# Expert layers of a tuned transformer kernel: a gather in fp32 straight from x, a fifth weight unit held aside, logits by token tiles, the gate bias as one row, and a last norm by halves

## The reference

```
x   = layer_norm(ALPHA * x + mix @ w_o[i])
aff = softmax(x @ router_w[i])                     # 256 tokens x 16 experts
gates, idx = top_k(aff.T, 32)                      # each expert takes its 32 best tokens
xg  = x[idx]                                       # 16 experts x 32 tokens
ffn = scatter_add(gates * ((silu(xg @ w1) * (xg @ w3)) @ w2))
ple = sigmoid(x @ ple_gate_w[i] + ple_gate_b[i]) * (p[i] @ ple_w[i])
x   = layer_norm(ALPHA * x + ffn + ple)
```

## Time and profile before

| | us |
|---|---|
| median of 3 runs | 2186.15 (2185.86 to 2186.26) |
| the profiled execution, its own time | 2185.28 |
| its span, first to last instruction | 2183.3 |
| PE busy | 1911.9, 88% |
| DVE, ACT busy | 1059.3, 712.3 |
| HBM read | 621.76 MB, 285 GB/s over the span |
| expert layer 0, in the profile | from about 128 to 609 |
| expert layer 1 | from about 711 to 1190 |

### The profile page before, as it was taken

One profiled execution on the slowest core, in us unless ns is written; L12 is line 12 of the kernel. 1 busy time (PEld: TensorE's weight loads), 2 busy tenths in 40 slices (PEclk: granted clock), 3 DMA queues, 4 the chain that ended last, 5 costly groups with the idle time before them and its releaser, 6 DMA issues. The chain is left out here.

```text
span 2183.3 us, 32580 instructions
## 1 busy us (share of the span) xinstructions
PE 1911.9 (88%) x13124; PEld 1354.3 (62%) x13140; DVE 1059.3 (49%) x1607; ACT 712.3 (33%) x1096; POOL 75.6 (3%) x137
## 2 busy tenths in 40 slices
PE   9999667676788986676768999999999999999998
PEld 6765224232366542242324888988888888888887
DVE  4761002010077500020103877787777877787776
ACT  5532002020046210020102433565444433565442
POOL 0000000000010000000000000000000000000000
PEclk9999989998999998898999999999999999999999
DMA  7399999999982899999999655436564655446550
GB/s 243 139 381 427 428 428 423 429 424 427 421 343 72 353 426 430 427 424 428 424 428 398 226 177 205 139 136 212 178 206 155 212 174 201 146 136 207 180 201 19
DMA packets 187952, 624.05 MB, mean 286 GB/s; under 512 B 17655, under 2 KB 129369, under 8 KB 163033
## 3 DMA queue, kind: packets, MB, share of 16 engines
q1 hardware_dynamic: 187864, 622.84, 73.6%
HBM read 621.76 MB, written 1.05 MB: 285 GB/s over the span
## 5 line engine op out<-in xcount | busy, mean ns | idle before, releaser
L3028 PE MATMUL psum<-x_both,up_hi 128*128 128x512 f32 x1408 | 352.9, 393 | 2.5 <-DVE x_both L525 2.2
L2275 PE MATMUL psum<-weight_ring,arena 128*32 128x256 f32 x3840 | 249.5, 411 | 106.7 <-DMA weight_ring<-in_w 106.1
L3028 PEld LDWEIGHTS psum<-x_both,up_hi 128*128 128x128 f32 x1408 | 257.4, 188 | 57.4 <-issue 3.3
L2275 PEld LDWEIGHTS psum<-weight_ring,arena 128*32 128x32 f32 x3840 | 123.5, 116 | 233.8 <-DMA weight_ring<-in_w 133.5
L2415 DVE TENSOR_TENSOR arena<-arena,psum 128x256 f32<-128x256 f32 x32 | 13.5, 421 | 450.6 <-PE psum L2275 450.6
L2297 PE MATMUL psum<-weight_ring,arena 128*32 128x512 f32 x1024 | 148.0, 709 | 73.6 <-DMA weight_ring<-in_w 63.6
L3080 DVE TENSOR_TENSOR up_lo<-weight_ring,up_hi 128x2048 fp32r<-128x2048 f32 x84 | 192.1, 2287 | 13.0 <-ACT up_hi L3051 12.8
L3031 PEld LDWEIGHTS psum<-x_both,up_lo 128*128 128x128 f32 x1408 | 189.4, 188 | 13.5
L3031 PE MATMUL psum<-x_both,up_lo 128*128 128x256 f32 x1408 | 193.2, 280 | 0.0
L3092 DVE TENSOR_REDUCE arena<-psum 128x256 f32<-128x512 f32 x176 | 121.5, 690 | 125.3 <-PE psum L3031 124.2
L652 PE MATMUL psum<-w_lo,x_both 128*128 128x384 f32 (+3 forms) x768 | 170.2, 359 | 2.4 <-DVE mix_lo L793 1.2
(11 more groups left out here) (390 smaller groups left out, 2393.7 us busy)
## 6 DMA issues: line engine op xcount, KB each, us to landing
weight_ring<-in_w SPq DMA_DIRECT2D x184, 2048.0 KB, 25.7
weight_ring<-in_ffn_wg SPq DMA_DIRECT2D x44, 1024.0 KB, 6.0
weight_ring<-in_ffn_wu SPq DMA_DIRECT2D x44, 1024.0 KB, 8.6
weight_ring<-in_ffn_wd SPq DMA_DIRECT2D x44, 1024.0 KB, 5.0
weight_ring<-in_w_in SPq DMA_DIRECT2D x14, 1536.0 KB, 6.7
weight_ring<-in_w_o SPq DMA_DIRECT2D x4, 2048.0 KB, 16.2
arena<-in_w SPq DMA_DIRECT2D x4, 2048.0 KB, 14.9
weight_ring<-in_ple_gate_w SPq DMA_DIRECT2D x4, 2048.0 KB, 25.0
```

The costliest lines, as they stand in the source:

```text
L2275: last = pe.matmul(ps[j * CAP:(j + 1) * CAP, 4 + k // 2, 0:QW], tokens[:, cc, :], w[c][:, j * QW:(j + 1) * QW], start=cc == 0, stop=cc == ...
L3028: last = pe.matmul(ps[:, 4 + 2 * f + h, :], w_part[:, f, h, c, :], x_both[:, :, c, :], start=c == 0, stop=False, skip_group_check=True)
```

## The change

Five edits. The gathers take x itself, in fp32, with eight elements between neighbours in the stationary operand, and one-hot matrices read as fp32; the first gather repeats its 64 columns twice, not four times. rows_hi and rows_lo are gone, and x_cols and ln_params hold a fifth aside unit, the first down unit of expert 1. Aside unit 0 is issued in `mix_out_norm`; the places of the ple inputs in the arena are moved for that. The columns for the logits are made tile by tile, and each tile has 24 products of 128 columns; two of the four ple products are made before them and two in the wait for the ranks. The gate bias is one row of 4 KB, which PE adds by a product with a row of ones ahead of the gate's products. The last norm has a root for each tile, halves of 512 columns, one of four on ACT, and four stores. Some semaphores are shared under one name by stages that don't overlap; no wait changes by that.

```diff
-FIRST, ASIDE = 2, 4
+FIRST, ASIDE, SPARE_PART = 2, 5, 3
...
@@ mix_out_norm, SP
             load_params(sp, (p_tokens, t["p"][layer, 0].rearrange("(a p) d -> p a d", p=P)))
+            sp.dma_start(Arena(0).take(SLOT), stream.aside[layer][0]).then_inc(signal("aside_unit_0_arrived").sem, 16)
             stream.issue(sp)
...
@@ experts
-                        [spare_unit[:, :]]]
+                        [spare_unit[:, :]],
+                        [x_cols.rearrange("p c q -> p (c q)"), ln_params.rearrange("p k n -> p (k n)")]]
...
+        def turn_tile(pe, a):
+            tile_ready(pe, a)
+            for half in range(2):
+                for c in range(DC // 2):
+                    cc = half * DC // 2 + c
+                    last = pe.transpose(tile_bank(a, half)[:, c, :], x[:, a, cc * P:(cc + 1) * P], ident[:, :])
+                last.then_inc(tile_turned.sem, 1)
+
+        def keep_tile_high(act, a):
+            for half in range(2):
+                act.wait_ge(tile_turned.sem, tile_turned.at(2 * a + half + 1))
+                act.copy(tile_columns(gate_hi, a, half), tile_bank(a, half)).then_inc(tile_high.sem, 2)
+
+        def keep_tile_low(dve, a):
+            for half in range(2):
+                dve.wait_ge(tile_high.sem, tile_high.at(2 * (2 * a + half + 1)))
+                dve.tensor_tensor(tile_columns(gate_lo, a, half), tile_bank(a, half),
+                                  tile_columns(gate_hi, a, half).bitcast(F32), ALU.subtract).then_inc(columns_made.sem, 2)
+
+        def logit_products(pe, a):
+            passes = ((router_hi, gate_hi), (router_hi, gate_lo), (router_lo, gate_hi))
+            for c in range(DC):
+                if c % (DC // 2) == 0:
+                    pe.wait_ge(columns_made.sem, columns_made.at(2 * (2 * a + c // (DC // 2) + 1)))
+                for k, (w_part, x_part) in enumerate(passes):
+                    last = pe.matmul(ps[0:EXPERTS, LOGIT_BANK, a * P:(a + 1) * P], w_part[:, c, :],
+                                     x_part[:, c, a * P:(a + 1) * P], start=c == 0 and k == 0,
+                                     stop=c == DC - 1 and k == len(passes) - 1)
...
+        @block.tensor
+        def _(pe):
+            ple_products(pe, (0, 1))
+            pe.wait_ge(summed_rows.sem, summed_rows.at(0))
+            idle_products(pe, 6, 3)
+            turn_tile(pe, 0)
+            idle_products(pe, 6, 3)
+            turn_tile(pe, 1)
+            pe.wait_ge(router_low_kept.sem, router_low_kept.at(1))
+            for a in range(TILES):
+                logit_products(pe, a)
...
@@ gate_products
+            params_ready(pe)
+            for a in range(TILES):
+                pe.matmul(ps[:, 6 + a, :], ident[0:1, 0:1].broadcast_to([1, P]), bias[0:1, h * BANK:(h + 1) * BANK],
+                          start=True, stop=False)
...
@@ gate_values
-            for a in range(TILES):
-                dve.tensor_tensor(ps[:, 6 + a, :], ps[:, 6 + a, :], bias[:, cols], ALU.add).then_inc(biased.sem, 1)
...
@@ gather_first
-            for part in (rows_hi, rows_lo):
-                for a in range(TILES):
-                    for c in range(DC):
...
+            for a in range(TILES):
+                for c in range(DC):
+                    last = pe.matmul(first_chunks[:, c, 0:REPEATS], in_chunks(x[:, a, :])[:, :, c],
+                                     one_hot[:, a, 0:FIRST * CAP].bitcast(F32).rearrange("p (u s) -> p u s", u=1)
+                                     .broadcast_to([P, REPEATS, FIRST * CAP]),
+                                     start=a == 0 and c % 2 == 0, stop=a == TILES - 1, skip_group_check=True)
...
@@ gather
-                    for part in (rows_hi, rows_lo):
-                        last = pe.matmul(ps[:, c % 4, :], part[:, a, c * P:(c + 1) * P], one_hot[:, a, :],
...
+                    last = pe.matmul(ps[:, c % 4, :], in_chunks(x[:, a, :])[:, :, c], one_hot[:, a, :].bitcast(F32),
+                                     start=a == 0, stop=a == TILES - 1)
...
@@ experts, SP
-            stream.issue(sp, early[0] + 6)
-
-            sp.wait_ge(used, ple_unit + 1)
+            stream.issue(sp, early[0] + 5)
+
+            sp.wait_ge(mixed.sem, mixed.at(0))
+            load_aside(sp, 4, 0)
             tile_ready(sp, 1)
...
+            load_aside(sp, 1, 0)
+            load_aside(sp, 4, 1)
+            sp.wait_ge(logit_rows.sem, logit_rows.at(1))
+            load_aside(sp, 2, 0), load_aside(sp, 2, 1)
+            issue_early(sp)
...
-            sp.wait_ge(gathered.sem, gathered.at(DC + 1))
+            sp.wait_ge(aside_used.sem, aside_used.at(ASIDE))
...
@@ experts, PE
-            idle_products(pe, 20)
+            ple_products(pe, (2, 3))
+            idle_products(pe, 2, 0)
...
@@ final_norm, POOL and DVE
+            for a in range(TILES):
+                root = roots[:, a:a + 1]
+                pool.wait_ge(squared.sem, squared.at(2 * a + 2))
+                pool_chain.link(pool, pool.tensor_scalar(root, half_sums[:, a, 0:1], half_sums[:, a, 1:2], EPS * D,
+                                                         ALU.add, ALU.add))
+                pool.tensor_tensor(root, root, half_power[:, 0:1], ALU.pow).then_inc(rooted.sem, 1)
...
+            dve.tensor_tensor(gained, half(x, 1, 0), half(ln_params, 0, 0), ALU.mult).then_inc(gains.sem, 1)
+            for a, h in by_vector:
+                dve.wait_ge(rooted.sem, rooted.at(a + 1))
+                dve.scalar_tensor_tensor(out=half(normed, a, h), in0=half(x, a, h), scalar=roots[:, a:a + 1],
+                                         in1=half(ln_params, 0, h), op0=ALU.mult, op1=ALU.mult
```

More of the change, by code:

```diff
@@ L2187, in before_columns, with tile_bank @@
[L2187 to L2194, removed]
+        tile_turned, tile_high = signal("columns_turned"), signal("columns_high_kept")
+        LOGIT_BANK = 5
+        def tile_bank(a, half):
+            return ps[:, 2 * a + half, :].rearrange("p (c q) -> p c q", c=DC // 2)
@@ L2277, in up, with down @@
                 last.then_inc(aside_used.sem if k < aside else used, 1)
[L2279 removed]
+        def down(pe, slot_unit, arrival, at, zeros=0, aside=4):
             pe.wait_ge(hid.sem, at(hid, 1))
@@ L2292, in down @@
                     more_zeros(pe, zeros)
-                w = stream.slot(slot_unit + 4 + k).rearrange("p (r h n) -> p r h n", r=4, h=2)
-                pe.wait_ge(stream.arrived[(slot_unit + 4 + k) % WEIGHT_SLOTS], arrival(slot_unit + 4 + k))
+                if 4 + k < aside:
+                    w = [part[:, r * D:(r + 1) * D].rearrange("p (h n) -> p h n", h=2) for part in aside_places[4 + k]
+                         for r in range(part.shape[-1] // D)]
+                    pe.wait_ge(aside_arrived[4 + k].sem, aside_arrived[4 + k].at(16 * len(aside_places[4 + k])))
+                else:
+                    unit = place_of(slot_unit + 4 + k)
+                    slot = stream.slot(unit)
+                    w = [slot[:, r * D:(r + 1) * D].rearrange("p (h n) -> p h n", h=2) for r in range(4)]
+                    pe.wait_ge(stream.arrived[unit % WEIGHT_SLOTS], arrival(unit))
                 for h in range(2):
@@ L2595, in _ @@
             pe.wait_ge(part_1.sem, at[0](part_1, 1))
-            down(pe, early[1], arrived_early, at[1])
+            down(pe, early[1], arrived_early, at[1], aside=ASIDE)
             gather(pe, range(6, DC))
@@ L2705, in _ @@
             make_hot(dve, range(FIRST))
-            low_row(dve, 0, 1)
-            for half in range(2):
-                low_row(dve, 1, half)
             make_hot(dve, range(FIRST, EXPERTS))
@@ L3779, in final_norm @@
     def final_norm(block):
-        normed = Arena().take(TILES, D)
+        normed, gained = Arena().take(TILES, D), Arena(TILES * D).take(BANK)
         roots = square_roots
-        rooted, done, stored = (signal(s) for s in ("root_ready", "tokens_scaled", "output_stored"))
+        rooted, gains, stored = (signal(s) for s in ("root_ready", "tokens_gained", "output_stored"))
+        vector_done, scalar_done = signal("vector_halves_scaled"), signal("scalar_half_scaled")
+        half = lambda tile, a, h: tile[:, a, h * BANK:(h + 1) * BANK]
+        by_vector = [(0, 0), (0, 1), (1, 1)]
         @block.sync
```

159 lines of the change are left out of this document (74 added, 85 removed).

## The result

The changed kernel is slower: 2192.16 us median of 14 runs (2187.90 to 2199.02) against 2185.38 of 14 (2182.84 to 2187.77) for the kernel before, 1.0032 times the time, 95% interval 1.0024 to 1.0039. Forecast was 2181.5. The profiled execution took 2187.90 us, span 2186.1, and is the fastest of the 14.

A forecast was written before the change was run, and what follows sets the result against it. Expert layers were taken as bound by the weight stream at 428 GB/s. Gains of 1.7 (layer 0), 0.9 (layer 1) and 2.0 us (last norm) summed to 4.6: median 2181.5 us, 2178 to 2185 by its own bounds, overall range 2173 to 2193.

The forecast's parts named there:

- I take no surcharge: First gather: reading x eight elements apart costs nothing extra, 3.8 us in all; other end, twice the time, 3.5 us a layer.
- rival (b): First gather's strided loads of x are dear: 3.5 us a layer on the path to the experts, 2188.6 us; chance 0.13.
- Logits by tiles: Logits made per token tile, 48 products of 128 columns at 0.06 us, last at 140.1: gain 0.9 us.
- rival (a): Narrow logits products are dear, 0.23 us each: 11.0 us in place of 2.9, 8.1 a layer, 2197.8 us; chance 0.16.
- Other gathers: Gathers after the first, four fp32r products a chunk become two fp32: 13.8 us in place of 7.9, loss of 5.9.
- U issued: U, the loops' first ring weight unit, waits for expert 2's first up quarter: issued at 195.6 and 778.85, from 190.83 and 774.05.
- Landing: Time from issue to landing of the loops' first ring unit: 8.1 us, the lower end, so 203.7 and 786.95.
- Slack: How much earlier the loops' first ring unit could have landed in the kernel before: 6.5 and 5.7 us.
- U's landing is the layer's shift: Stream is unbroken behind the loops' first ring unit, so its landing shifts the expert layer equally: gains 1.7 and 0.9 us.
- Last norm: Kernel's end: a root per tile, halves and four stores finish near 2181.0 instead of 2183; gain 2.0 us, bounds 1.2 and 2.6.
- Gate bias: Expert loops: four fp32 products on PE (3.4 us a layer) replace four DVE additions; zero, as PE idles there.
- split rows removed: Beside ranking or gather: DVE loses four subtractions, ACT two casts; zero, up to 0.3 us gained.

The follow-up runs named there:

- e1: Changed kernel, but both gathers read 128 neighbouring elements of x, so the experts get the columns in another order: 2185.23 us, ratio to before 0.9994.
- s1: Changed kernel with the first gather's stationary elements 4 apart (16 bytes) in x tile 0 and 2 apart (8 bytes) in tile 1: one execution, 2189.91 us.
- s2: Changed kernel, first gather in products of 64 stationary columns, step 8 elements in x tile 0 and 4 in tile 1: one execution, 2183.38 us.
- s3: Changed kernel with its own columns and one edit, first gather in products of 64 stationary columns at a step of 8 elements: 2185.10 us, ratio 1.0001.
- n1: Kernel before plus 24 idle bf16 products (5.2 us of PE) per expert layer, directly ahead of expert 2's up products: 2185.10 us, ratio 0.9994.
- n2: Kernel before plus 48 idle bf16 products (10.4 us of PE) per expert layer, directly ahead of expert 2's up products: 2193.85 us, ratio 1.0034.
- k2: Changed kernel with packed copies of x's rows, expert 2's tokens in the first gather, two other gather chunks behind expert 2's up products: 2185.43 us, ratio 0.9994.
- k3: As k2, with four of eight other gather chunks behind expert 2's up products, two each between up and down of experts 0 and 1: 2184.18 us, 0.9995.
- e3: Kernel before with only the changed last norm, by halves: 2183.59 us, ratio 0.9995.
- e4: Changed kernel with the gathers, split rows and four aside units of the kernel before: 2186.62 us, ratio 1.0006.
- the later set: The changed kernel unchanged, run again beside other kernels on the same chip and profiled a second time: 2194.43 us (4 runs), ratio 1.0041.

## Why the prediction was wrong

The step that failed is the one on the first gather's strided operand that ends in "I take no surcharge". The price was 4.04 us a layer (7.88 against 3.84 in e1), above even the other end of 3.5, and it is the mechanism of rival (b), which had a chance of 0.13. What the step was built on was a row with the right step of 16 bytes but loads of 64 columns; in s1 128 columns at that step cost double, in s2 and s3 loads of 64 columns had no such price at 16 or 32 bytes. The nearest row was near in one dimension and not in the other. The Trainium skill, SBUF — State Buffer (Specifications (TRN2)), says that full bandwidth wants at least two hits in a line of 16 bytes. By that rule a step of 8 bytes is free and 16 and 32 are not; for loads of 128 columns s1 agrees (0.117 at 8 bytes, 0.233 at 16), and so does the changed kernel (0.238 at 32); for loads of 64 columns no run agrees (0.06 at 16 and 32). The rule stood against the change and my own row was allowed to silence it.

Rival (b)'s price was too low all the same (2188.6). The other sizes, by the forecast's own steps:

- *Logits by tiles*, −0.9 forecast, −1.2 and −0.85 measured at layer 0's first gather in the two profiles. 0.06 a product, right; rival (a) is out.
- *Other gathers*, +5.9 forecast, +6.6 measured. e1 has U 4.4 us earlier than the changed kernel behind the first gather's start, of which 4.04 is that gather itself: 0.4 of the missing 0.7 is the stride here too. The other 0.3 goes with the three groups, which in e1 take 0.1 to 0.2 us each beyond 0.86 a product; the sum left that out.
- *U issued* 195.6 and 778.85 forecast, 200.16 and 784.18 measured. In layer 0 the 4.6 us are 4.1 from the first gather (7.88 for 3.8) and 0.7 from the others, less 0.3 from the logits. *Landing* 8.6 and 8.9 for 8.1. So U came at 208.8 in place of 203.7, and the sign turned.
- *Slack*: 6.5 and 5.7 us. n1 and n2 bear it out: 5.2 us moved V by 0.7 and 0.6 and cost no time that shows, 10.4 moved V by 4.3 and 5.1. This part of the argument was right, and with PE 9.3 to 10.5 us late it gives a loss of 3.4 to 5.
- *U's landing is the layer's shift*: true as long as U is the last late unit, as in the changed kernel. It is no rule: V decided in k2 and k3, and in layer 1 of s3 U landed as before (55.0 against 54.9 behind the first gather) but V 1.7 us later.
- *Last norm*, −2.0 forecast, −1.0 measured. POOL's first step of tile 1's root took 1.35 us in place of 0.31, from 2180.13 to 2181.48, just while DVE ran its two halves, 2179.99 to 2181.40. In e3 the same step took 1.35 too. The Trainium skill, SBUF — State Buffer (Terms), has the two engines share one pair of ports, locked for a whole instruction; the rows agree in that POOL's step ended only behind DVE's, but it was behind two instructions of DVE, and no run here took DVE's halves away from that place. The sum had tile 1's root ready 1.6 us behind the last half of x, whatever DVE did; DVE's last half, which waited for it, started 2.9 us behind.
- *Gate bias*, *split rows removed*, *ple products late*: nothing forecast. They were not taken one by one; e4, which keeps the first and the last, is within its interval level with the kernel before, though it also has the last norm's gain.

With the sizes measured the sum is 3.4 for layer 0, 4.3 for layer 1 (5.3 at U, less 1.0 that came in from layer 0's end) and −1.0: 6.7 us, and 6.8 were measured. That the two meet so closely is luck: the interval goes from 5.2 to 8.5, and the later set gave 9.2.

The loss hangs on one price of 4 us a layer, laid on a lead of six. The forecast gain needed more than its absence. e1 and s3 are without that price, and both are level with the kernel before (0.9994 and 1.0001), not 4.6 us under it. In s3 U was issued at 196.6 in layer 0, not at 195.6, took 8.8 us to land, not 8.1, and landed at 205.35, where it had landed before the change (205.38), not at 203.7; V landed 1.0 and 1.7 us later behind the first gather than before. So two smaller steps of the sum failed as well: the lower end of the landing times, and U's landing taken for the layer's shift.

## What to carry to other kernels

Where a ring of weights runs ahead of the compute, draw up the lead: for each slot, when it is freed, plus what a load into an empty queue takes (7 to 9 us here), against when its unit could have landed in a full queue. Here work inside the lead was free and work beyond it cost in full; work that is moved must be followed to the last slot that it makes late, not to the first. Take a row for another operation only if step and width of its operand both agree; where only one does, the other end of the bound is a case with real weight.

## What the runs showed of the hardware

- Loads of 128 fp32 columns into PE, each with a product of 128 moving columns: 0.111 us a record packed (e1), 0.117 with 8 bytes from one element to the next (s1), 0.233 with 16 (s1), 0.238 with 32 (changed kernel). Loads of 64 columns: 0.06 a record with 16 and 32 bytes (s2). Splitting each strided load in two took the first gather from 7.88 to 4.12 us with the same columns (s3).
- Fp32r products of 128 columns with 16 stationary columns stand 0.06 us apart (changed kernel), half of the 0.117 that those of 256 columns stand apart before.
- ACT's copy of 128 x 1024 with a step of 32 bytes took 2.1 us in e2; in the changed kernel its two casts of 512 columns out of PSUM (L2195) took 1.07 together.
- A 2 MB load issued more than a microsecond after the queue had run empty landed 7.2 to 9.2 us after its issue. U in layer 1 took 7.2 us in n2, where the queue had been empty for 1.6 us, and 7.2 in s3 and 8.9 in the changed kernel, where it was issued 0.7 us before the unit ahead of it had landed.
